# First context pass of a two-layer transformer block: merge and out units as rounded products of split weights, rope read from PSUM, gate Sigmoids moved behind the attention loop

## The reference, cut to what matters

```python
h = modulate(rmsnorm(x, norm1_g[l]), sh1, sc1); p = h @ w_in[l]
q, k, v = ...                                   # q = rope_2d(q), k = rope_2d(k): latents only
y_conv = silu(layernorm(dwconv1d(a * sigmoid(g), dw))) @ w_conv_out
y_attn = merge_heads(attention(q, k, v, k_ctx, v_ctx)) @ w_na_out
g_conv, g_attn = split(sigmoid(p[..., QKV_END:]))
x = x + g1 * ((g_conv * y_conv + g_attn * y_attn) @ w_out[l])
x = x + g2 * conv_ffn(modulate(rmsnorm(x, norm2_g[l]), ...))
```

## Time and profile before

| | us |
|---|---|
| median of three runs | 2962.23 |
| lowest, highest | 2959.38, 2964.63 |
| profiled execution, its own time | 2951.68 |
| its span, first to last instruction | 2949.4 |
| TensorE busy (PE) | 2816.3 |
| DVE busy | 1537.3 |
| POOL busy | 1274.6 |
| ACT busy | 1116.2 |
| mean granted clock of TensorE | 0.981 |

### The profile page before, as it was taken

The page is one execution under the profiler, slowest core; times in us unless marked ns, Lnnn a source line. Parts: engine busy times, 40 slices in busy tenths (PEclk is TensorE's granted clock), DMA queues, the critical chain, the costliest instruction groups (busy, mean ns, idle before and its releaser), DMA issues.

```text
span 2949.4 us, 41217 instructions
## 1 busy us (share of the span) xinstructions
PE 2816.3 (95%) x15658; PEld 2297.0 (78%) x15658; DVE 1537.3 (52%) x1968; ACT 1116.2 (38%) x1666; POOL 1274.6 (43%) x696
## 2 busy tenths in 40 slices
PE   7999988999999999989999999999989999999998
PEld 6975734878888877867777888888877777788887
DVE  6865585353323255278775432423355867552525
ACT  4445223333323233236633422322343573342433
POOL 3444101435445173388842322222347784444443
PEclk9999998999999999999999999999999999999999
DMA  4235497323233233432222212122223222333332
GB/s 174 95 101 212 135 314 250 95 93 100 91 95 99 93 123 122 143 93 83 68 86 65 72 55 74 57 65 65 72 86 114 76 68 72 100 93 94 99 94 78
DMA packets 116008, 306.88 MB, mean 104 GB/s; under 512 B 36176, under 2 KB 44496, under 8 KB 115344
## 3 DMA queue, kind: packets, MB, share of 16 engines
q1 hardware_dynamic: 87584, 284.49, 30.5%
q10 hardware_dynamic: 27712, 18.50, 2.2%
q0 software_dynamic: 560, 1.84, 0.2%
HBM read 294.95 MB, written 7.45 MB: 103 GB/s over the span
## 4 chain that ended last, share of the span: by engine, by line
PE 77%; DVE 8%; DVEq 4%; ACT 3%; issue 2%; POOL 2%; DMA 2%; ACTq 1%; SPq 0%; POOLq 0%
PE ps L304 38%; PE ps L338 17%; PE ps L329 6%; PE ps L1941 3%; DVEq L2241 2%; POOL wlo L265 2%; DVE co L2240 2%; PE ps L2352 2%; PE ps L1945 1%; PE ps L1946 1%; PE ps L1949 1%; DMA mt<-ka 1%; PE ps L748 1%; DVE nacc L451 1%; PE ps L1999 1%
## 5 line engine op out<-in xcount | busy, mean ns | idle before, releaser
L265 POOL TENSOR_TENSOR wlo<-wraw,whi 128x1024 fp32r<-128x1024 f32 x373 | 923.1, 2484 | 1360.7 <-ACT whi L257 1359.3
L257 ACT ACTIVATE whi<-wraw 128x1024 fp32r<-128x1024 f32 x373 | 392.3, 1055 | 458.2 <-PE ps L304 170.5
L304 PE MATMUL ps<-xah,whi 128*128 128x512 f32 x992 | 387.9, 391 | 1.7 <-issue 1.7
L304 PE MATMUL ps<-xal,whi 128*128 128x512 f32 x992 | 387.4, 391 | 0.0
L304 PE MATMUL ps<-xah,wlo 128*128 128x512 f32 x992 | 280.1, 391 | 0.0
L2240 DVE SCALAR_TENSOR_TENSOR co<-ub,vec,co 128x512 f32<-128x512 f32 (+1 forms) x216 | 247.7, 1186 | 5.4 <-issue 0.4
L304 PEld LDWEIGHTS ps<-xah,whi 128*128 128x128 f32 x992 | 186.1, 188 | 42.8 <-issue 2.7
L304 PEld LDWEIGHTS ps<-xal,whi 128*128 128x128 f32 x992 | 186.1, 188 | 40.3
L304 PEld LDWEIGHTS ps<-xah,wlo 128*128 128x128 f32 x992 | 186.1, 188 | 40.2
L2339 POOL TENSOR_TENSOR co<-co,ct 128x512 f32<-128x512 f32 (+1 forms) x144 | 168.1, 1167 | 21.7 <-issue 1.8
L304 PE MATMUL ps<-hhi,whi 128*128 128x512 f32 x408 | 159.3, 390 | 1.1 <-ACT whi L257 1.1
(11 more groups left out here) (419 smaller groups left out, 6065.1 us busy)
## 6 DMA issues: line engine op xcount, KB each, us to landing
wraw<-stream SPq DMA_DIRECT2D x425, 512.0 KB, 3.5
wada<-w_ada SPq DMA_DIRECT2D x56, 512.0 KB, 7.4
wraw<-w_ada SPq DMA_DIRECT2D x40, 512.0 KB, 3.9
biasb<-attn_bias ACTq DMA_DIRECT2D x32, 256.0 KB, 3.6
xin<-x0T SPq DMA_DIRECT2D x4, 528.0 KB, 6.7
s_u<-uk ACTq DMA_DIRECT2D x8, 264.0 KB, 2.5
res<-x0T ACTq DMA_DIRECT2D x1, 2048.0 KB, 9.5
outT<-res SPq DMA_DIRECT2D x4, 512.0 KB, 2.6
```

Of the source, the lines that this page charges most:

```text
L257: act.activation(whi[:, s], wraw[:, s], ACT.Copy).then_inc(hi_done[s], 1)
L265: pool.tensor_tensor(wlo[:, s], wraw[:, s], whi[:, s].bitcast(F32), ALU.subtract).then_inc(lo_done[s], 1)
L304: last = pe.matmul(ps[:, bank, 0:b - a], w[:, s, kt], x[:, kt, c0 + a:c0 + b], start=start, stop=stop)
```

## The change

- c0: `N_WHOLE` is 36, `N_CTX = 52`; units 36 to 51 of c0 (merge and out) are split units. Their activations are split: attention outputs, the four tiles behind Silu, the eight merged tiles (`m1`, `h1` go). Squares and sums of `l0a` move from the merge to the out units; its rows move behind the second unit after the out quad, its root on ACT behind four roundings.
- Rope: the sine product goes back into PSUM bank 3 in place, not to `rt`; the mixed windows of keys are summed once more from PSUM instead of copied from kT, and those of v are copied from PSUM instead of from vT; one drain less in each.
- Late Sigmoids: the ten gates in the attention loop are evacuated by Copy and get their Sigmoid in place beside units U+29 to U+33, in all three passes.
- Merge order: the layer norm uses bank (U+3) % 4; in the quad the fourth unit starts last, and units 1 to 3 are counted ahead of its four lo products.
- c1: the root stands behind the first copy.
- Filler products: 8 in front of the last turn of the S5 stage, 4 in front of the SSD out units.

```diff
-N_WHOLE = 52
+N_WHOLE = 36
+N_CTX = 52
@@ def s5_pe(pe): @@
             if i in ADA_END:
                 pe.wait_ge(f_a.sem, f_a.past("bat", min(i + 2, NT - 1)))
+                if i == NT - 1:
+                    keep_busy(pe, 1, 8)
                 ada_turn(pe, ADA_END[i])
@@ def kv_act(act, p, then): @@
-        norm_root_act(act, n, then.T, "eps6")
         for j in range(4):
...
             act.activation(kctx[:, j], ps[:, s, 0:p.T], ACT.Copy).then_inc(acc_free[s], 1)
+            if j == 0:
+                norm_root_act(act, n, then.T, "eps6")
             split_hi(act, p.U + j + R)
@@ def evac_act(act, p, g): @@
-            act.activation(gt[:, h, 0:p.T], a, ACT.Sigmoid).then_inc(acc_free[s], 1)
+            act.activation(gt[:, h, 0:p.T], a, ACT.Sigmoid if g >= p.U + 30 else ACT.Copy).then_inc(acc_free[s], 1)
@@ def mix_act(act, p): @@
         for g in range(p.U + 29, p.U + 36):
             evac_act(act, p, g)
+            d = 2 * (g - p.U - 29)
+            for h in range(d, min(d + 2, 30 - GATE0)):
+                act.activation(gt[:, h, 0:T], gt[:, h, 0:T], ACT.Sigmoid)
...
-                act.activation(h1[:, m, 0:T], lsq[:, m, 0:T], ACT.Silu, bias=colr(f"lnb{p.l}", 1, m)).then_inc(p.c_h.sem, 1)
-                continue
@@ def post_dve(dve, p, i): @@
-                dve.drain()
                 for m_, (lo, hi) in MIX.items():
-                    dve.tensor_copy(vT[0:64, m_], vT[0:64, lo])
-                    ins = dve.tensor_copy(vT[64:P, m_], vT[64:P, hi])
+                    dve.tensor_copy(vT[0:64, m_], v[0:64, lo - 2])
+                    ins = dve.tensor_copy(vT[64:P, m_], v[64:P, hi])
...
-            dve.tensor_tensor(rt[:, :], ps[:, 3, :], sinT, ALU.mult)
+            t = ps[:, 3, :]
+            dve.tensor_tensor(t, t, sinT, ALU.mult)
             dve.drain()
             if k == 0:
-                ins = dve.tensor_tensor(bycol(qT[:, :]), grid(x), grid(rt[:, :]), ALU.add)
+                ins = dve.tensor_tensor(bycol(qT[:, :]), grid(x), grid(t), ALU.add)
             else:
+                def keys(at, c, n):
+                    o = kT[:, at:at + GH * n].rearrange("p (c r) -> p c r", r=GH)
+                    return dve.tensor_tensor(o, grid(x)[:, c:c + n], grid(t)[:, c:c + n], ALU.add)
+
                 for a in range(2):
...
-                dve.drain()
+                    keys(4 * P * a, 32 * a, 32)
                 for m_, (lo, hi) in MIX.items():
-                    dve.tensor_copy(kT[:, m_ * P:m_ * P + 64], kT[:, lo * P:lo * P + 64])
-                    ins = dve.tensor_copy(kT[:, m_ * P + 64:m_ * P + P], kT[:, hi * P + 64:hi * P + P])
+                    keys(m_ * P, 16 * (lo - 2), 8)
+                    ins = keys(m_ * P + 64, 16 * hi + 8, 8)
@@ def merge_pe(pe, p): @@
         attention_hi(M)
-        pe.wait_ge(acc_free[M % R], read_out(M - R))
+        pe.wait_ge(acc_free[(M + 3) % R], read_out(M - 1))
         conv_mean_pe(pe, p)
...
-            for kt in range(4):
-                last = lo_part(0, kt)
-            counted(0, last)
-            for j in range(1, R):
-                counted(j, lo_part(j, 3))
+        for j in range(R - 1):
+            counted(j, lo_part(j, 3))
+        for kt in range(4):
+            last = lo_part(R - 1, kt)
+        counted(R - 1, last)
@@ def out_context_act(act, p, then): @@
+        for kt in range(NT):
+            norm_square(act, n, kt, then.src, then.T, lambda e, kt: e.wait_ge(n_fin.sem, n_fin.past("fin", NT - 1)))
+        for m in range(R):
+            split_hi(act, p.U + 44 + m + R)
         norm_root_act(act, n, then.T, "eps6")
@@ def out_context_dve(dve, p, then): @@
-        norm_rec_dve(dve, n, then.T)
+        for kt in range(NT):
+            norm_add(dve, n, kt, then.T)
         add = lambda m: add_unit_dve(dve, p.U + 44 + m, 0, 0, m, p.res, p.T, p.modv(2))
         for m in range(R):
             add(m)
+        norm_rec_dve(dve, n, then.T)
@@ TensorE's order @@
             ssd_pe(pe)
+            keep_busy(pe, 5, 4)
             raw_pe(pe, U_OUT1, "ssd", hhi, hlo, lambda: raw_sums_ssd(pe), lambda: s5_first_pe(pe))
...
-                    pe_quad(pe, p.U + 44, 0, 0, m1, mlo, p.T, hi=lambda pe, kt: pe.wait_ge(p.m_w.sem, p.m_w.past("w", kt)))
-                    norm_rows_pe(pe, passes[1].norm(0), SEQ)
+                    pe_quad(pe, p.U + 44, 0, 0, mhi, mlo, p.T, hi=lambda pe, kt: pe.wait_ge(p.m_h.sem, p.m_h.past("hi", kt)),
+                            lo=lambda pe, kt: pe.wait_ge(p.m_l.sem, p.m_l.past("lo", kt)))
                     for j in range(R):
-                        pe_unit(pe, p.U + 48 + j, 0, 0, m1, mlo, p.T)
+                        pe_unit(pe, p.U + 48 + j, 0, 0, mhi, mlo, p.T)
+                        if j == 0:
+                            norm_sums_pe(pe, NORM["l0a"], SEQ)
+                        if j == 1:
+                            norm_rows_pe(pe, passes[1].norm(0), SEQ)
```

More of the change, by code:

```diff
@@ L2273, in mix_dve @@
                 scale_dve(dve, p, n)
-            if out_due(p, n) is not None and not p.one:
+            if out_due(p, n) is not None:
                 out_lo_dve(dve, p, out_due(p, n))
@@ L2331, in mix_pool @@
         for k in range(1, p.taps):
-            if p.U + 11 + k < p.U + 40:
+            if not p.one and p.U + 11 + k < p.U + 40:
                 split_lo(pool, p.U + 11 + k)
@@ L2341, in mix_pool @@
         pool.drain()
-        for g in range(p.U + 11 + p.taps, p.U + 40):
+        for g in range(p.U + 36 if p.one else p.U + 11 + p.taps, p.U + 40):
             split_lo(pool, g)
@@ L2354, in attention_hi @@
         def attention_hi(g):
-            if p.one:
-                here(pe, g, 0, 0)
-                for kt in range(4, 8):
-                    product(g, wraw, hh, kt, start=kt == 4, stop=kt == 7)
-                return
             hi_split(pe, g, 0, 0)
@@ L2385, in hi_part @@
         def hi_part(j, kt):
-            if p.one:
-                return product(M + j, wraw, hh, kt, start=kt == 0, stop=kt == 3)
             product(M + j, whi, hhi, kt, start=kt == 0)
@@ L2397, in merge_pe @@
         all_freed(pe, M)
-        for kt in range(4):
+        for kt in range(2):
             pe.wait_ge(p.c_h.sem, p.c_h.past("hi", kt))
-            for j in range(1, R):
-                last = hi_part(j, kt)
-                if p.one and kt == 3:
-                    counted(j, last)
+            for j in range(R - 1):
+                hi_part(j, kt)
+            if kt:
+                pe.wait_ge(p.c_lo.sem, p.c_lo.past("lo", 0))
+                for j in range(R - 1):
+                    lo_part(j, 0)
@@ L2404, in merge_pe @@
+        for kt in range(2, 4):
+            pe.wait_ge(p.c_h.sem, p.c_h.past("hi", kt))
+            for j in range(R - 1):
+                hi_part(j, kt)
             if kt == 2:
                 pe.wait_ge(p.c_n.sem, p.c_n.past("n", 3))
[L2406 to L2415 removed]
@@ L2416, in merge_pe @@
-        if not p.one:
-            pe.wait_ge(p.c_lo.sem, p.c_lo.past("lo", 3))
-            for kt in range(4):
-                last = lo_part(0, kt)
-            counted(0, last)
-            for j in range(1, R):
-                counted(j, lo_part(j, 3))
-        def summed(m):
-            if p.one:
-                pe.wait_ge(p.m_w.sem, p.m_w.past("w", m))
-            else:
-                pe.wait_ge(p.m_v.sem, p.m_v.past("v", m))
+                hi_part(R - 1, 0)
+                hi_part(R - 1, 1)
@@ L2429, in merge_pe @@
+            hi_part(R - 1, kt)
+            pe.wait_ge(p.c_lo.sem, p.c_lo.past("lo", kt - 1))
+            for j in range(R - 1):
+                lo_part(j, kt - 1)
+        pe.wait_ge(p.c_lo.sem, p.c_lo.past("lo", 3))
+        for j in range(R - 1):
+            counted(j, lo_part(j, 3))
+        for kt in range(4):
+            last = lo_part(R - 1, kt)
+        counted(R - 1, last)
         for j in range(4):
-            pe_unit(pe, M + R + j, 0, 0, hh, hlo, p.T, dual=True, half=lambda: summed(j))
@@ L2431, in merge_pe, with merge_act @@
-        if p.one:
-            summed(R + 2)
-            norm_sums_pe(pe, NORM["l0a"], SEQ)
+            pe_unit(pe, M + R + j, 0, 0, hhi, hlo, p.T, dual=True, half=lambda: pe.wait_ge(p.m_v.sem, p.m_v.past("v", j)))
     def merged(p, m):
         return mv[:, m % 2, 0:p.T] if m < R else ps[:, R + (p.U + m) % R, 0:p.T]
-    def merge_act(act, p, then=None):
-        if p.one:
-            for kt in range(NT):
-                norm_square(act, then.norm(0), kt, then.src, then.T, lambda e, kt: e.wait_ge(n_fin.sem, n_fin.past("fin", NT - 1)))
-            return
+    def merge_act(act, p):
@@ L2461, in merge_dve @@
             s, rnd = slot(p.U + 36 + m)
-            if p.one:
-                norm_add(dve, then.norm(0), m, then.T)
             dve.wait_ge(unit_done[s], rnd + 2)
@@ L2474, in merge_dve @@
                 lo(m - 1)
-        if not p.one:
-            lo(NT - 1)
+        lo(NT - 1)
     def ffn_units(p):
@@ L3002, in _ @@
                     mix_pool(pool, p)
```

(1 more changed line is left out.)

84 lines of the change are left out of this document (25 added, 59 removed).

## The result

| | before | changed |
|---|---|---|
| median of the runs made with the result, us | 2960.81 (4) | 2939.20 (4) |
| lowest, highest | 2956.88, 2964.63 | 2935.80, 2939.82 |
| profiled execution | 2951.68 | 2938.65 |
| its span | 2949.4 | 2936.8 |
| mean granted clock | 0.981 | 0.979 |

Ratio 0.9925, 95% interval 0.9908 to 0.9942: faster, by 0.75%, clear of the noise. The forecast of 2941.2 is 2 us off. But the two profiles lie only 13 us apart where the medians lie 21.6 apart, so a sum of terms made on a profile can't have been right for its own reasons alone. The rest of this text is mostly about that. One of the ten executions in experiment 3 ran in a slow state (3517.6 us, granted clock 0.745) and is left out of its median there.

A forecast was written before the change was run, and what follows sets the result against it. TensorE was taken to bound the kernel, three quarters of the chain that ended last. Terms +4.5 - 6 - 8 - 3.7 - 3.3 - 1 - 2.5 - 1 = -21.0 gave 2930.7, with the 10.5 offset 2941.2; range 2926 to 2956.

The forecast's parts named there:

- (a): c0, conv branch's layer norm: variance 3.2 later, then a quad of 5.7 instead of 7.16, ending at 1166.9 instead of 1166.3.
- (b): c0, GpSimd: eight splits back to back at 2.5, the eighth done at 1188, pace the out quad, which ends at 1198.9.
- (c): c0, norm of l0: sums behind the fifth and rows behind the sixth out unit, so scaling begins at 1206.5 instead of 1203.04.
- (d): l0's start: first product 14.7 behind scaling's start, at 1221.2, 3.4 later than before; TensorE idles 9 us, low clock follows.
- The first rival: c0: the norm does not decide, c0 gives -5.6 to -6.5, total -32, 2930; chance 0.10.
- Rope and key posts: l0 and l1: a key post shrinks by some 3 us, waits for keys and the low clock go; -6 and -8.
- Late Sigmoids: Late steps of l0 and l1: fourteen or so table loads leave the loop, freeing TensorE's pex waits; -3.7 and -3.3.
- Order: Merge of both latent passes: unit 1 counted three products earlier, a wait of 0.53 goes; -1 together.
- Root: Last context pass: TensorE's 1.57 wait for the rounding goes and GpSimd's six splits start earlier; -2.5, between -1.6 and -3.5.
- Fillers: Eight in the S5 stage against a low clock: -1, between +1 and -2.2; four before the SSD out units: 0.
- GpSimd's taps as the end of both passes: Latent passes: loops stay as long, GpSimd's taps let through only some 3 us each; total -6, 2956; chance 0.16.
- A further held tap in each late step: Late steps of the latent passes: one more tap held, 2.0 each, 32 in 16 steps; with all, 2973; chance 0.06.

The follow-up runs named there:

- experiment 3: Changed kernel, rounded c0 kept, with l0's norm sums put into the out quad and its rows straight behind it: 2935.68 us, ratio 0.9947 to the kernel before.
- the second comparison: Changed kernel run again without an edit, against the kernel before in a later set: 2939.81 us, ratio 0.9944 (0.9924 to 0.9964).
- the mixed one: Changed kernel with c0's merge units rounded, its out units plain, and the norm's squares and sums in the merge: 2939.71 us, ratio 0.9932.
- experiment 9: Changed kernel with c0's merge units rounded and out units plain, 2939.71 us, beside the changed kernel with all of c0 plain, 2929.71 us.

## Why the prediction was right, and where not

**The total** was right with the help of luck, by errors of opposite sign. The sum of the terms was -21.0, but what the change does from c0 on is -12.8 to -15.6 by the profiles. And the offset of 10.5 between the profiled execution and the median of three runs, carried over as if it belonged to the kernel, belonged to that sample. Set against the medians of later sets (2952 to 2960), -14 would give 2938 to 2946, and the changed kernel is at 2939 to 2940. A part stays open. A gain of 14 lies inside the interval of the second comparison (11 to 22 us) and outside that of the first (17 to 27), and no stretch of the profiles shows the 5 to 7 us by which the medians lie further apart.

**The context pass**: the mechanism was right in steps (a) to (c), and in (d) in part; the size was not: +4.5 foretold, +6.8 to +8.1 in c0's stretch, inside the bound of +9, and with the low clock in l0 late (1.6, foreseen by no term) 8.4 to 9.7. The misses are small and add up. (a) ended 3.5 late. Its 3.2 for the variance was exact (1155.30 before, 1159.11 now, with c0 begun 0.65 later), but 1166.3 + 3.2 - (7.16 - 5.7) is 1168.0 and not 1166.9: 1.1 was lost in the addition. The rest is the 0.65, and a low clock from 1160 to 1167 that the working did not foresee: the quad ran 6.83, not 5.7, and the products ahead of it 0.7 longer. (b) and (c) kept that delay to within a tenth or two. (d) The first product was 2.4 late against 1221.2. The 14.7 that the working took for the scaling was read wrongly: in the kernel before TensorE came to that product straight from its out units, so the row shows only that the scaling takes no longer. In the changed kernel, where TensorE does wait, 13.8 pass from the first scaled tile to the product, ScalarE's rounding included. The low clock lay from 1218.3 to 1228.5, so 4.9 us of it behind the first product, which costs 2.4 where I counted 1.1. The first rival, that the norm doesn't decide, is out by experiment 3: the earlier norm gives 2.4 to 3.1. What else decides differs by kernel. In the changed one the chain has GpSimd's eight remainders, from 1171.66 to 1191.41 without a gap, but no run varied their number alone. In the mixed one it was DVE's sums between the merged tiles, and with these behind them and the out units plain the stretch is 12.4 to 13.1 shorter than in the changed kernel.

**Rope and key posts**: -6 and -8 foretold; l0 early is 6.6 shorter, l1 early 7.5 on the mean of before, each the same in all kernels that have this part. The working had a post 3 us shorter; the rows give 2 x 0.60 for the sums, 4 x 0.58 in copies against 4 x 0.25 in sums, some 2.5, and a drain. The working put it to the copies and the drains, and bounded the sums of 256 and 64 columns at 1.7 together; they take 2 x 0.618 + 4 x 0.252 = 2.2. What it did not see is that the old sums were held by GpSimd like the taps. One reason was wrong: the low clock in l0 (0.91 over 20 us) cost nothing, for the profile of the kernel before again shows a clock of 1.00

```profile
1284.00:1304.00 20.00, 15.88 (x72) 11.73 (x70) 15.15 (x18) 6.18 (x10) 18.52 (x13) 1.00 0.26 71
```

at the same post, and "l0 early" is 57.1 us there against 57.0: TensorE was waiting for DVE, at either clock. The Trainium skill (VectorE: DVE Perf Modes, section on the TRN2 errata) was cited for a higher fixed cost of a PSUM source; the rows show the sums faster by half, and a difference as small as the fixed costs can't be seen beside it. The page that bears on it is another: SBUF — State Buffer, section Who interferes with whom, says that a DVE instruction with two inputs in SBUF contends with a GpSimd instruction that reads SBUF, and one with at most one such input outside the two-port modes doesn't. By 1218 and 618 ns for the same sum, and by the 1.55 and 0.69 of experiment 9, the traces agree.

**Late Sigmoids**: -3.7 and -3.3 foretold. With rope in place 3.2 and 3.7 to 5.3, and 1.6 in the order stretch, where a low clock follows the wait for lmu. The loads went as foretold (one for Exp is left in each latent loop). The further 1380 ns that the prediction sets beside a load are not in the trace: a load at 1154.99 takes 1.28, and ScalarE's next instruction starts at 1156.29. The size is right, the step is not: "what they can free is TensorE's wait for pex" fails, as these waits stayed at 4.7 and 4.8. The path is DVE's wait for exp, then its last tap, then the wait for lmu; of this one the prediction had no term, though the kernel before shows it in l0:

```profile
PE ps L2309 <- DVE lmu L2286: 3.3, 1, 3.3
```

**Small parts.** Order: -1 foretold, 0.7 in l0; right. Root: -2.5 foretold, 0.3 at most; the step that failed is that a root behind the first key copy frees the rounding. It still stood ahead of the rounding and waited for the norm's sums, so TensorE waits 1.3 instead of 1.57, and GpSimd's remainders follow that rounding. Fillers: -1 foretold for those in front of the S5 turn, 0 for those at the SSD out units; nothing can be told. The clock window that priced them was 0.78 in one execution and, as the kernel before again shows, 1.00 in the next:

```profile
514.00:524.00 10.00, 8.78 (x37) 6.97 (x38) 2.17 (x11) 0.63 (x1) 2.61 (x2) 1.00 0.64 238
```

**The other rivals.** GpSimd's taps as the end of both passes: no, in the latent passes of the changed kernel TensorE runs into the merge without waiting for lmu. A further held tap in each late step: no sign of it.

## What to carry to other kernels

A faster form of the products is worth what the engines that feed it can keep up with: splitting sixteen units was to save TensorE 10.6 us of its own work and made the stage 7 to 8 longer; splitting eight of them, with one engine's sums moved out of the way, made it 5 shorter. Where DVE is on the path and GpSimd works beside it, look first for its instructions with two inputs in SBUF, and leave one of them in PSUM. Before a wait is moved, look for what the instruction that ends it waited for itself. And before a difference of 10 us is explained, profile the unchanged kernel twice and subtract stretch by stretch.

## What was not expected of the hardware

- The kernel before differs by 16 to 23 us between executions of one set, 0.5% to 0.8%; in the profiles most of it lies in the first 530 us, where TensorE's clock falls at different places (0.88 or 1.00 over 55 us). What decides that, and why the median of the kernel before was 2952 in one set and 2959 to 2960 in others, each on another chip, stays open.
- A DVE copy of 64 columns from SBUF to SBUF took 0.62 on the mean beside GpSimd's taps and 0.18 at its shortest, a sum of the same 64 columns with one operand in PSUM 0.25.
- A table load on ScalarE (1.28) that is hidden for TensorE is not hidden for DVE, whose reciprocal waits for the exp: 6.3 us of it in one latent pass.
